# A hybrid encoder layer on one core: the attention stage written as a pipeline over head pairs, with z tiles in front of it and a DeltaNet tile behind it

## The reference

```
h = rms_norm(x, norm1_g);  proj = h @ w_in            # 2048 columns in
q_lat, kv_lat, k_rope, qkv, z, a_f, a_b, b_f, b_b = split(proj)
# group A, 8 heads of attention
q  = rms_norm(q_lat) @ w_q_b      # 8 heads x (128 nope + 64 rope)
kv = rms_norm(kv_lat) @ w_kv_b    # 8 heads x (128 k_nope + 128 v)
k  = concat(k_nope, k_rope shared by all heads)
q, k = rms_norm(q), rms_norm(k);  the 64 rope columns are rotated
mla_out = softmax(q k^T / sqrt(192)) v                # within each token group
# group B, 8 heads of bidirectional gated DeltaNet on silu(conv(qkv)),
# gated by silu(z): gdn_out
x = x + concat(mla_out, gdn_out) @ w_o
x = x + expert_choice_moe(rms_norm(x, norm2_g))       # 16 experts
```

## Time and profile before

| | |
|---|---|
| median of 3 runs | 3655.47 us (3647.66 to 3660.75) |
| the profiled execution | 3650.89 us, its span 3649.1 us |
| busy in the span | PE 3351.3 us (92%), DVE 915.6 (25%), ACT 479.5 (13%), POOL 260.3 (7%) |
| window 340 to 380 (z) | PE busy 40.0 of 40 us |
| window 380 to 396 (border) | PE busy 0.58 of 16 us |
| window 475 to 554 (a head pair) | PE busy 69.77 of 79 us, DVE 34.82, ACT 29.50, POOL 9.72 |
| window 760 to 850 (first DeltaNet tiles) | PE busy 90.0 of 90 us |

### The profile page before, as it was taken

The page is one execution under the profiler, slowest core; times in us unless marked ns, Lnnn a source line. Parts: engine busy times, 40 slices in busy tenths (PEclk is TensorE's granted clock), DMA queues, the critical chain, the costliest instruction groups (busy, mean ns, idle before and its releaser), DMA issues. The chain is left out here.

```text
span 3649.1 us, 29486 instructions
## 1 busy us (share of the span) xinstructions
PE 3351.3 (92%) x11460; PEld 1795.9 (49%) x11460; DVE 915.6 (25%) x1549; ACT 479.5 (13%) x1225; POOL 260.3 (7%) x328
## 2 busy tenths in 40 slices
PE   6899788799999999988599975999999999999998
PEld 3454344355776767757444444333433333333333
DVE  1100344322654655657300024000000000000000
ACT  2210233302113122131100010000000000000000
POOL 0000111100200202112000000000000000000000
PEclk8999899899999999988799985999999999999999
DMA  4110100120111111000341024888888888888884
GB/s 154 46 48 18 48 23 31 48 75 23 47 53 58 43 45 47 12 20 21 117 177 48 0 92 161 345 314 317 315 311 314 314 314 314 312 321 315 317 311 155
DMA packets 157786, 551.36 MB, mean 151 GB/s; under 512 B 9519, under 2 KB 42119, under 8 KB 135047
## 3 DMA queue, kind: packets, MB, share of 16 engines
q1 hardware_dynamic: 153607, 525.02, 39.7%
q0 software_dynamic: 4096, 25.17, 3.1%
HBM read 515.47 MB, written 34.70 MB: 151 GB/s over the span
## 5 line engine op out<-in xcount | busy, mean ns | idle before, releaser
L1878 PE MATMUL psum<-ring,xeT 128*96 128x512 f32 x2048 | 884.4, 594 | 2.0 <-ACT h L1929 1.3
L1878 PEld LDWEIGHTS psum<-ring,xeT 128*96 128x96 f32 x2048 | 334.5, 163 | 548.4 <-issue 547.4
L1896 PE MATMUL psum<-ring,hT 128*96 128x512 f32 x1024 | 442.2, 592 | 1.4 <-ACT hT L1924 0.7
L979 PE MATMUL psum<-xT,wg 128*128 128x512 f32 x768 | 356.3, 600 | 13.6 <-DMA wg<-in_w_in 13.6
L1617 PE MATMUL psum<-wo,mixT 128*128 128x512 f32 x768 | 331.6, 594 | 22.9 <-DMA wo<-in_w_o 22.1
L408 PE MATMUL psum<-wb,xT 128*128 128x512 f32 (+1 forms) x768 | 308.7, 562 | 0.0
L1896 PEld LDWEIGHTS psum<-ring,hT 128*96 128x96 f32 x1024 | 166.1, 163 | 265.8 <-issue 264.1
L1617 PEld LDWEIGHTS psum<-wo,mixT 128*128 128x128 f32 x768 | 146.4, 191 | 207.6 <-issue 206.0
L408 PEld LDWEIGHTS psum<-wb,xT 128*128 128x128 f32 x768 | 146.4, 192 | 153.7 <-issue 134.6
L1954 DVE COPY hT<-psum 128x384 f32<-128x384 f32 x16 | 8.9, 557 | 822.6 <-PE psum L1860 822.6
L979 PEld LDWEIGHTS psum<-xT,wg 128*128 128x128 f32 x768 | 140.4, 193 | 139.8 <-issue 137.8
(11 more groups left out here) (249 smaller groups left out, 2503.4 us busy)
## 6 DMA issues: line engine op xcount, KB each, us to landing
ring<-in_w_gate SPq DMA_DIRECT2D x64, 2048.0 KB, 7.2
ring<-in_w_up SPq DMA_DIRECT2D x64, 2048.0 KB, 9.5
ring<-in_w_down SPq DMA_DIRECT2D x64, 2048.0 KB, 8.2
wg<-in_w_in SPq DMA_DIRECT2D x12, 2048.0 KB, 8.7
wo<-in_w_o SPq DMA_DIRECT2D x4, 4096.0 KB, 15.1
wb<-in_w_in SPq DMA_DIRECT2D x3, 4096.0 KB, 14.9
rows<-gate_rows SPq DMA_DIRECT2D x48, 256.0 KB, 6.0
mixT<-mix SPq DMA_DIRECT2D x4, 1536.0 KB, 18.5
```

The costliest lines, as they stand in the source:

```text
L979: last = nc.tensor.matmul(ps[:, b, 0:SS_], wg[:, m % 2, d, h * P:(h + 1) * P], k.xT[:, d, SP_:T], start=(d == 0), stop=(d == KD - 1))
L1878: last = nc.tensor.matmul(ps[0:CT, 2 * (u // 4) + half, :], xeT[:, q, :], m[:, kk, 512 * half:512 * half + 512], start=(q == 0), stop=(q = ...
L1896: last = nc.tensor.matmul(ps[0:CT, 4 + q % 2, :], hT[:, f, :], m[:, f, :], start=(f == 0), stop=(f == 7))
```

## The change

In `latents` the last two z units (tiles 4 and 5 of the second half) are left out, SP stores only the rest, and requests the attention weights of pair 0 and, behind the last z store, the DeltaNet weights of pair 0's first two tiles. These weights and the z weights stay in one buffer, `wbuf`, through all three stages.

In `attention` the loops are written out. PE's order is: the six tiles of pair 0, the two z units (`last_z`), all transposes of pair 0, tile 0 of pair 1, and then 48 units over all pairs without a break. Between the scores and the transposed probabilities of a unit stands one piece of work of the next pair: a projected tile in steps 0 to 4, two batches of transposes in steps 5 to 10, and in step 11 tile 0 of the pair after it. In the last pair three passes (matmuls) of DeltaNet's tile 0 stand there (`first_qkv`). Projection and transposes share the two banks 5 and 6. The rotary parts of both heads are transposed together, so 16 batches become 12. v has a copy of its own (`vbuf`), in two buffers, so that kv is copied by two instructions. DVE, ACT and POOL get orders that match; POOL reuses its temporary tiles, with more waits between its instructions but as many of them. SP stores the two z tiles from the buffers of the probabilities.

In `deltanet` the projection starts with tile 1.

```diff
+    k.wbuf = sb("wbuf", [P, 2, KD, 512])
+    k.wg = k.wbuf[:, 0].rearrange("p k n -> p (k n)").rearrange("p (b k n) -> p b k n", b=2, k=KD)
+    k.s_half = k.sem("qkv_sample_projected", L)
+    k.s_proj = k.sem("qkv_projected", L)
+    k.s_wg = [k.sem("qkv_weights0", L), k.sem("qkv_weights1", L)]
...
+    k.wq = sm("wq", [P, 4, 2 * QH])
+    k.wkv = sm("wkv", [P, 2, 2 * (NOPE + VH)])
...
+                sp.dma_start(k.wq[:], a["w_q_b"][0].rearrange("(p k) n -> p k n", k=4)[:, :, 0:2 * QH]).then_inc(k.s_wa, 16)
+                sp.dma_start(k.wkv[:], a["w_kv_b"][0].rearrange("(p k) n -> p k n", k=2)[:, :, 0:2 * (NOPE + VH)]).then_inc(k.s_wa, 16)
...
-                    sp.wait_ge(s_z, NT * (half + 1))
-                    sp.dma_start(k.zs[:, :, 512 * half:512 * half + 512].rearrange("t p c -> p t c"),
-                                 zs[:, :, 512 * half:512 * half + 512]).then_inc(s_rows, 16)
+                    nt = NT - 2 * half
+                    sp.wait_ge(s_z, NT * half + nt)
+                    sp.dma_start(k.zs[0:nt, :, 512 * half:512 * half + 512].rearrange("t p c -> p t c"),
+                                 zs[:, 0:nt, 512 * half:512 * half + 512]).then_inc(s_rows, 16)
+                sp.wait_ge(s_acc, 3 * NT)
+                for j, kind in enumerate((1,)):
+                    c0 = C_QKV + kind * GW
+                    sp.dma_start(k.wg[:, j], a["w_in"][0].rearrange("(p k) n -> p k n", k=KD)[:, :, c0:c0 + 2 * P]).then_inc(k.s_wg[j], 16)
...
-                for v in range(2 * NT):
+                for v in range(2 * NT - 2):
...
-                for u in range(2 * NT + 3, 4 * NT):
+                for u in range(2 * NT + 3, 4 * NT - 2):
...
+    BATCHES = ([("q", h, b) for h in range(2) for b in range(2)] + [("k", h, b) for h in range(2) for b in range(2)]
+               + [("kr", 0, b) for b in range(2)] + [("qr", 0, b) for b in range(2)])
+    NB = len(BATCHES)
+    BY_ACT, BY_DVE = (0, 1, 2, 3, 10, 11), (4, 5, 6, 7, 8, 9)
+    last_unit = lambda g: max(u for u in range(NU) if 2 * units[u][0] + units[u][1] == g)
+    GROUP_END = {last_unit(g): g for g in range(4)}
...
+                def load_w(i):
+                    sp.wait_ge(s_pq, i * NT)
+                    sp.dma_start(wq[:], wq_d[:, :, i * 2 * QH:(i + 1) * 2 * QH]).then_inc(s_w, 16)
+                    sp.wait_ge(s_pkv, i * NT)
+                    sp.dma_start(wkv[:], wkv_d[:, :, i * 2 * (NOPE + VH):(i + 1) * 2 * (NOPE + VH)]).then_inc(s_w, 16)
+
+                load_w(1)
+                for m in range(2):
+                    sp.wait_ge(s_zg, m + 1)
+                    sp.dma_start(k.zs[NT - 2 + m, :, 512:1024], pr[:, m, :]).then_inc(s_out, 16)
+                for i in range(HP):
+                    if i + 2 < HP:
+                        load_w(i + 2)
+                    sp.wait_ge(s_mix, 4 * (i + 1))
+                    sp.dma_start(k.mix[2 * i:2 * i + 2].rearrange("h p t -> p h t"), mix_sb[:]).then_inc(s_out, 16)
+                sp.wait_ge(s_out, HP * 16 + 32)
...
+                def project(i, t):
+                    n = i * NT + t
+                    if t == 0:
+                        pe.wait_ge(s_w, 32 * (i + 1))
+                        if i:
+                            pe.wait_ge(s_ta, 6 * i)
+                    if t:
+                        pe.wait_ge(s_rq, n)
+                    for kk in range(4):
+                        last = nc.tensor.matmul(ps[:, 5, 0:2 * QH], k.qlT[:, kk, t * P:(t + 1) * P], wq[:, kk, :],
+                                                start=(kk == 0), stop=(kk == 3))
+                    last.then_inc(s_pq, 1)
+                    if t:
+                        pe.wait_ge(s_rkv, n)
+                    for kk in range(2):
+                        last = nc.tensor.matmul(ps[:, 6, :], k.kvlT[:, kk, t * P:(t + 1) * P], wkv[:, kk, :],
+                                                start=(kk == 0), stop=(kk == 1))
+                    last.then_inc(s_pkv, 1)
...
                 def transposes(i, b):
                     if b == 0:
-                        pe.wait_ge(s_mix, i * 4 + 4)
-                    elif 4 <= b < 8:
-                        pe.wait_ge(s_ta, i * 8 + (b - 3))
-                    elif b >= 8:
-                        wait_apart(pe, s_tv, i * 8 + (b - 7), k)
-                    if kind == "q":
-                        pe.wait_ge(s_raw, i * (2 * NT) + 2 * (3 * half + 3))
-                    elif b == 4:
+                        pe.wait_ge(s_rq, NT * (i + 1))
+                    elif b == 1:
+                        pe.wait_ge(s_rkv, NT * (i + 1))
+                    elif b < 6:
+                        pe.wait_ge(s_ta, 6 * i + b - 1)
+                    else:
+                        pe.wait_ge(s_tv, 6 * i + b - 5)
+                    if b == 4:
                         pe.wait_ge(s_kn, i + 1)
-                    elif b == 12:
-                        wait_apart(pe, s_qr, i + 1, k)
+                    elif b == 10:
+                        pe.wait_ge(s_qr, i + 1)
...
+                        last = nc.tensor.transpose(ps[:, 5 + b % 2, j * P:(j + 1) * P], src, k.ident)
...
+                def last_z(m):
+                    t = NT - 2 + m
+                    for d in range(KD):
+                        last = nc.tensor.matmul(ps[:, 2 + m, :], k.xT[:, d, t * P:(t + 1) * P], k.wbuf[:, 1, d, :],
+                                                start=(d == 0), stop=(d == KD - 1))
+                    last.then_inc(s_zp, 1)
+
+                def first_qkv(lo, hi):
+                    for step in range(lo, min(hi, 2 * KD)):
+                        d = step % KD
+                        if step == 0:
+                            pe.wait_ge(k.s_wg[0], 16)
+                            pe.wait_ge(s_ta, 6 * HP)
+                        c0, S = (SP_, SS_) if step < KD else (0, SP_)
+                        last = nc.tensor.matmul(ps[:, 5 + step // KD, 0:S], k.wg[:, 0, d, 0:P], k.xT[:, d, c0:c0 + S],
+                                                start=(d == 0), stop=(d == KD - 1))
+                        if d == KD - 1:
+                            last.then_inc(k.s_half if step < KD else k.s_proj, 1)
+
+                for t in range(NT):
+                    project(0, t)
+                last_z(0)
+                last_z(1)
+                for b in range(NB):
+                    transposes(0, b)
+                project(1, 0)
+                scores(0)
+                for n in range(N):
+                    i, u = divmod(n, NU)
+                    if u == 0:
+                        scores(n + 1)
+                        if n:
+                            values(n - 1)
+                    if u < NU - 2:
+                        scores(n + 2)
+                    if i + 1 == HP:
+                        first_qkv(3 * u, 3 * u + 3)
+                    elif u < 5:
+                        project(i + 1, u + 1)
+                    elif u < NU - 1:
+                        transposes(i + 1, 2 * u - 10)
+                        transposes(i + 1, 2 * u - 9)
+                    elif i + 2 < HP:
+                        project(i + 2, 0)
+                    if u == NU - 1 and i + 1 < HP:
+                        scores(n + 1)
+                    probs_t(n)
+                    if u and u - 1 in GROUP_END:
+                        values(n - 1)
+                values(N - 1)
...
+                def norm_k(i):
+                    dve.wait_ge(s_rs, i + 1)
+                    dve.wait_ge(s_rkv, i * NT + NT)
+                    if i:
+                        dve.wait_ge(s_tp, NB * i)
+                    rk = rs[:, i % 2, 2:4, :].rearrange("p h t -> p t h")
+                    nc.vector.tensor_tensor(kraw[:], kraw[:], bcast(rk, 3, NOPE), ALU.mult)
+                    nc.vector.tensor_tensor(krot[:], bcast(kg[:], 2, 2), bcast(rk, 3, ROPE), ALU.mult).then_inc(s_kn, 1)
+                    st.done(nc.vector.tensor_scalar(rs[:, i % 2, 0:2, :], rs[:, i % 2, 0:2, :], QH ** -0.5, None, ALU.mult))
...
+                for t in range(NT):
+                    copy_raw(0, t)
...
+                sum_squares(0)
+                norm_k(0)
+                for m in range(2):
+                    z = pr[:, m, :].rearrange("p (h c) -> p h c", c=P)
+                    dve.wait_ge(s_zs, m + 1)
+                    nc.vector.tensor_tensor(z, z, bcast(k.gng[:], 1, 4), ALU.mult).then_inc(s_zg, 1)
+                for b in BY_DVE:
+                    store(0, b)
+                copy_raw(1, 0)
+                for n in range(N + 3):
+                    i, u = divmod(n, NU)
+                    if n < N:
+                        maximum(n)
+                    if 1 <= n <= N:
+                        scale(n - 1)
+                    if n >= 3 and (n - 3) % NU in GROUP_END:
+                        mix(n - 3)
+                    if i + 1 < HP:
+                        if u <= 5 and n:
+                            copy_raw(i + 1, u)
+                        if u == 6:
```

(38 more changed lines are left out.)

417 lines of the change are left out of this document (185 added, 232 removed).

## The result

| | before | after |
|---|---|---|
| median, each of 4 runs | 3651.56 us (3647.24 to 3660.75) | 3603.38 us (3601.44 to 3604.14) |
| the profiled execution, its span | 3650.89, 3649.1 | 3604.14, 3602.3 |
| PE busy in the span | 3351.3 us, 92% | 3341.0 us, 93% |

The ratio is 0.9864 with a 95% interval of 0.9842 to 0.9886: faster by 1.4%. The forecast was 3607, its range 3583 to 3636. The medians differ by 48.2 us, the two spans by 46.8.

A forecast was written before the change was run, and what follows sets the result against it. PE, busy 92%, was taken as the engine whose idle time bounds the kernel. Gains 9.45 + 51.4 + 7.0 less waits 4.7, 16.5 and 1.0 make 45.7 us: 3605.2, stated as 3607, range 3583 to 3636.

The forecast's parts named there:

- The move up to 3607: Whole kernel: 3605.2 from the profiled execution, 3609.8 from the median of three runs; the prediction said 3607.
- Border one: Latents to attention: the weight wait goes and PE's 15.95 us idle becomes 6.5, a gain of 9.45.
- the 6 us bound: Start of attention: upper bound on delay from the 2 MB DeltaNet load queued behind the z transfer, if later transfers are late.
- The pair: Attention head pair: without waits and with 12 transpose batches for 16, 78.66 us becomes 65.8; four pairs save 51.4.
- First pair: Pair 0: z tiles cover k's norm, but table loads, silu and stores make transposes 9.5 us for 4.8, losing 4.7.
- Transitions: Steps 5 to 11 between pairs: new PE waits of 5.5 us each, 16.5 for three.
- the clock falls in the transposes: Rival: two-bank transpose batches lower the clock, 2.0 us in each of four stages, 3615; chance 0.22 together with Given back in the queues.
- the clock is at 0.5 outside the borders: Sign of a wrong prediction: granted clock at 0.5 (1.2 GHz) anywhere but at the stage borders.
- Border two: Attention to DeltaNet: the weight wait goes, PE's idle falls from 13.64 to 6.6 us, a gain of 7.0.
- Given back in the queues: Rival: DVE's order limits; transitions and last pair wait 9.2 us each, 3626; chance 0.22 together with the clock falls in the transposes.
- the idle only moves: Rival: each of the 48 units waits 0.95 us more, so the 45.7 us gain is gone, 3652; chance 0.04.
- Slower: Rival: clock swings through the whole stage; 311 us of work at 1.2 GHz takes 311 more, 3916; chance 0.04.

The follow-up runs named there:

- e1: The kernel before with only the two loads of the attention weights moved into latents: 3642.58 us for 3653.66, ratio 0.9973.
- e2: The changed kernel with the 2 MB load of the first DeltaNet weights requested inside attention, not behind the last z transfer of latents: 3599.81 us, ratio 0.9860.
- e4: The changed kernel with the two z tiles in front of pair 0's projections, not between them and its transposes: 3615.99 us, ratio 0.9911.
- e9: e6's order, DeltaNet tile 0's second half behind the last values, no memset wait on PE, ACT's first four stores between the silus: 3591.16 us, ratio 0.9821.
- e7: The changed kernel with POOL's rotation of q cut to two of its seven instructions per pair: 3595.25 us, ratio 0.9825.
- e5: The changed kernel with the next pair's first scores in step 11 ahead of the projected tile, not behind it: 3601.60 us, ratio 0.9848.
- e10: The changed kernel again, unaltered, on the same chip as e9: 3602.19 us, ratio 0.9851.
- e6: e5's order with three passes of DeltaNet's tile 0 in the empty step 11 of the third transition, later passes three earlier: 3598.47 us, ratio 0.9833.
- e8: e6 plus second z tile spread between pair 0's transposes, half of DeltaNet's tile behind the last values, no memset wait on PE: 3590.69 us, ratio 0.9816.
- e3: The changed kernel with all 32 matmuls of DeltaNet's tile 0 behind the last attention values, none in the last pair: 3599.59 us, ratio 0.9858.
- e11: The changed kernel without PE's wait for three memsets before the first DeltaNet matmul: 3602.17 us, ratio 0.9851.

## Why the prediction was right

**Direction, size and place** held: 3603.4 for 3607, and 46.8 by the spans for a sum of 45.7. Against its own execution the sum gave 3605.2 and the profiled execution took 3604.1. The move up to 3607 leant on the median of three runs, 3655.5; with one run more it is 3651.6.

**Border one.** Held: 6.95 for 6.5, and e1 shows that the load was 8.3 of the gain. The 2 MB behind the z store cost 0.25 (e2), so the 6 us bound was far out.

**The pair.** Held best in its work: 65.61 for 65.8. With its waits it is 69.37, just under the 70 to 72 that the prediction asked for. Of the 78.66 - 65.61 = 13.05 gained, 9.2 are waits and 3.5 are transposes (the six double batches last 0.71 + 0.87 + 0.88 + 0.76 + 0.72 + 1.01 = 4.95 us for 8.44); this split is read from the traces, as no run takes one part of the pipeline away. That k's norm hides behind transposes and values from the second pair on is in the list of waits, where the 23.2 has gone.

**First pair.** 9.41 for 9.5 (10.1 in the executions where the clock fell there), and the cover's value is shown by e4: without it 12.66 of wait. That ACT's table load and silus sit in front of the first store is right; e9, with the first stores between the silus, has 0.34 there in place of 1.93.

**Transitions.** The step that was mis-sized: 5.5 each, measured 3.76. Forecast and measured by place: 0.8 and 0.54 for the scale that POOL delays (step 6, ahead of the norm), 0.6 and 0.58 for the probabilities behind the norm (7), 0.5 and nothing behind the k stores (8), 1.2 and 0.84 (10), 0.9 and 0.49 (11, ACT's store), 1.5 and 1.31 (11, the maximum). So the kinds of wait were right, and e7 and e5 confirm the first two and the last. The largest miss is step 8, where two k stores of 0.57 stand in front of the next maximum and PE does not wait at all; ACT's store and step 10 make 0.4 each, POOL's scale 0.3, the maximum 0.2. The norm's 5.2 us was read from rows beside POOL and came out at 5.26, with POOL beside it again; e7 shows that it is 2.88 without. Over three transitions the sum was 5.2 us too careful.

**The clock.** The rival *the clock falls in the transposes* came in small part. In the profiled execution of the change it did not happen in pair 0's batches: the windows from 414 to 428, with waits up to 1.93, all grant 1.00. But in e10, the same kernel, it did, as in five other runs, for 0.7 us where the rival charged 2.0 a stage. And a dip came at the end of the sparse third transition, for 3.1 us, where the sum had nothing. The prediction named "the clock is at 0.5 outside the borders" as a sign of being wrong; by this sign it was wrong on the clock, although the size of it, 2.6 us against the sum, left the total near. A filler in the third transition keeps the clock up in e6 and e8 and not in e9. The Trainium skill, "TensorE: Matmul & The Clock Gate", section "A second HAM failure mode: psum-queue depth-cycling", describes short pauses between groups of matmuls, with PSUM banks cycled through, as a cause; the traces agree that no wait above 2 us is needed, but with the same batches the clock falls in one execution and not in another.

**Border two.** Held, 6.49 for 6.6. What the prediction did not ask is whether DeltaNet's tile serves better behind the last values. It does: 2.26 (e3), and 0.32 with half of the tile there and the memset wait gone too (e9). What of the wait is memsets, 1.9 of 6.49, is shown by e11.

**Errors that cancel.** +5.2 in the transitions and -2.6 in the clock are the two of size; every other term is within 1 us. The total was near partly for that reason, which is luck.

**The other rivals.** *Given back in the queues* (9.2 a transition) is excluded by 3.76; *the idle only moves* by steps 0 to 4 of each pair, which have no wait. *Slower* would have needed most of the stage at the low level; some 6 us inside it had it, and 3 to 5 at work behind each border.

**Open.** Why the clock falls in one execution and not in another of the same order (the first transition in e3, e10 and e11, pair 0's batches in six runs) was not settled. The six in which it fell in pair 0's batches are all among the eight with the slow first q (5.46); whether the one brings the other no run shows.

## What to carry to other kernels

When a pipeline hides a wait, ask of each filler what it covers: the z tiles cover 11 us of another engine's chain, DeltaNet's tile inside the last pair 0.7, and the same tile behind it 4.2 of a stage change. A duration read beside POOL holds POOL's delay already, so ask whether POOL will stand beside it in the new order too. Where dense work ends, look at the granted clock and not at the waits alone, and in more than one execution: one profile without a dip doesn't exclude it.

## What the runs showed of the hardware

- A product of one column on DVE takes 0.16 us, and 1.39 when it began 0.43 us into a POOL instruction of 1.81, with which it ended; DVE's norm takes 5.26 beside POOL and 2.88 without (the change, e7).
- The clock fell to 1.2 GHz for about 6 us after 4 us in which PE was busy 2.29, in short passes, no wait being longer than 1.3 (the change). Twelve batches of transposes with waits up to 1.93 and PE busy 50 to 85% of the 2 us windows from 416 to 426 did not bring it down in the change and e2; the same batches did in e3, e5, e6, e7, e10 and e11, at a cost of 0.7 us.
- After a border gap of 6.7 to 7.1 us the first eight q passes took 4.21 and 4.29 in two executions (the change, e2) and 5.46 in eight (e3, e5 to e11).
- A stage change on PE costs 0.32 us when PE itself ends the stage last and the transfer is over (e9: the mix transfer is issued at 684.58 and such a transfer lands after 3.4, PE starts the next stage at 691.05).
